# Sums of weight blocks moved from VectorE to DMA transfers that add to their destination

## The reference, cut to what matters

```python
def swiglu(x, g, w_gate, w_up, w_down):
    n = rms_norm(x, g)
    return (jax.nn.silu(n @ w_gate) * (n @ w_up)) @ w_down
# D_MODEL = 1024, D_FF = 2816, DEPTH = 2; x is 512 + 128 rows
```

## Time and profile before

| | |
|---|---|
| median of three runs | 1427.65 us (1426.31 to 1430.56) |
| profiled execution, its time | 1429.83 us |
| its span in the trace | 1428.5 us |
| TensorE busy | 98% of the span |
| VectorE busy | 74% |
| ScalarE busy | 50% |
| GpSimd busy | 11% |
| granted TensorE clock | full in every slice |
| RUN, layer 0 and 1 | 376.4 to 676.7 us; from 1076 to 1375 us |

### The profile page before, as it was taken

One profiled execution on the slowest core, in us unless ns is written; L12 is line 12 of the kernel. 1 busy time (PEld: TensorE's weight loads), 2 busy tenths in 40 slices (PEclk: granted clock), 3 DMA queues, 4 the chain that ended last, 5 costly groups with the idle time before them and its releaser, 6 DMA issues.

```text
span 1428.5 us, 24281 instructions
## 1 busy us (share of the span) xinstructions
PE 1402.7 (98%) x9340; PEld 1321.5 (93%) x9340; DVE 1061.1 (74%) x1875; ACT 713.0 (50%) x1414; POOL 156.6 (11%) x110
## 2 busy tenths in 40 slices
PE   7999999999999999999999999999999999999998
PEld 6897878999999999999988978699999999999998
DVE  5658667878789889877444776677797998998853
ACT  5458555334355455454444685643344544544534
POOL 2416020210000000000222341102000000000002
PEclk9999999999999999999999999999999999999999
DMA  5330221233022222322233211213221223222312
GB/s 171 109 113 14 74 70 39 81 104 104 30 89 66 89 84 74 104 89 74 74 84 107 85 56 47 77 42 102 79 74 60 82 71 114 62 88 89 111 45 96
DMA packets 148642, 115.25 MB, mean 81 GB/s; under 512 B 17936, under 2 KB 143248, under 8 KB 148496
## 3 DMA queue, kind: packets, MB, share of 16 engines
q1 hardware_dynamic: 148528, 113.71, 26.4%
HBM read 108.90 MB, written 6.62 MB: 81 GB/s over the span
## 4 chain that ended last, share of the span: by engine, by line
PE 86%; DVE 7%; ACT 3%; DMA 1%; issue 1%; SPq 1%; DVEq 0%; ACTq 0%
PE ps L675 23%; PE ps L1359 13%; PE ps L1360 13%; PE ps L1361 13%; PE ps L802 3%; PE ps L804 3%; PE ps L803 3%; PE ps L1236 1%; PE ps L1127 1%; ACT pw L1521 1%; PE ps L728 1%; DMA wraw<-w_uq 1%; DVE ringl L2507 1%; PE ps L917 1%; PE ps L1153 1%
## 5 line engine op out<-in xcount | busy, mean ns | idle before, releaser
L2037 DVE TENSOR_TENSOR wlo<-wraw,whi 128x1024 fp32r<-128x1024 f32 (+2 forms) x87 | 97.6, 1122 | 122.9 <-ACT whi L1475 122.8
L1360 PE MATMUL ps<-tl,ringh 128*128 128x320 f32 x576 | 177.8, 309 | 0.0
L1361 PE MATMUL ps<-tth,ringl 128*128 128x320 f32 x576 | 177.5, 308 | 0.0
L1359 PE MATMUL ps<-tth,ringh 128*128 128x320 f32 x576 | 177.0, 307 | 0.0
L1891 ACT ACTIVATE ringh<-sums 128x512 fp32r<-128x512 f32 (+1 forms) x208 | 123.7, 595 | 106.3 <-DVE sums L2499 35.9
L2507 DVE TENSOR_TENSOR ringl<-sums,ringh 128x512 fp32r<-128x512 f32 (+1 forms) x208 | 134.2, 645 | 9.6 <-ACT ringh L1891 8.2
L1475 ACT ACTIVATE whi<-wraw 128x1024 fp32r<-128x1024 f32 (+2 forms) x87 | 81.0, 936 | 112.5 <-PE ps L675 52.0
L1360 PE MATMUL ps<-tbl,ringh 128*128 128x320 f32 x432 | 133.5, 309 | 0.0
L1361 PE MATMUL ps<-tbh,ringl 128*128 128x320 f32 x432 | 133.4, 309 | 0.0
L1359 PE MATMUL ps<-tbh,ringh 128*128 128x320 f32 x432 | 133.4, 309 | 0.0
L1359 PE MATMUL ps<-dhi,ringh 128*128 128x320 f32 x336 | 105.6, 314 | 5.2 <-DVE dlo_rest L2512 2.8
(11 more groups left out here) (431 smaller groups left out, 3786.4 us busy)
## 6 DMA issues: line engine op xcount, KB each, us to landing
raw_gate<-w_gate SPq DMA_DIRECT2D x18, 1024.0 KB, 5.4
raw_up<-w_up SPq DMA_DIRECT2D x18, 1024.0 KB, 5.3
raw_gate<-w_down SPq DMA_DIRECT2D x8, 768.0 KB, 4.2
raw_up<-w_down SPq DMA_DIRECT2D x8, 768.0 KB, 4.2
wraw<-w_down SPq DMA_DIRECT2D x16, 384.0 KB, 3.3
wraw<-w_out SPq DMA_DIRECT2D x32, 128.0 KB, 2.9
wraw<-w_out SPq DMA_DIRECT2D x16, 256.0 KB, 3.1
wraw<-w_gate SPq DMA_DIRECT2D x8, 512.0 KB, 3.9
```

The lines of the kernel that those rows point to most:

```text
L1359: mm(o, wh[:, c, :], xh[:, c, :], start=fresh and c == 0, stop=False, skip_group_check=True)
L1360: mm(o, wh[:, c, :], xl[:, c, :], start=False, stop=False, skip_group_check=True)
L1361: ins = mm(o, wl[:, c, :], xh[:, c, :], start=False, stop=c == (DP if down else KH) - 1, skip_group_check=True)
L2037: vec.tensor_tensor(wlo[:, w], wraw[:, w], whi[:, w], ALU.subtract).then_inc(unit_lo.sem, 1)
```

## The change

All four sums of a set are made by DMA transfers that GpSimd issues and that add their source to what lies at their destination (`add_block`). Since such a transfer can only add, the sums are redefined without a minus, and the signs move to the right operands and to the emptying of PSUM:

- 5: a21 + a22, in the place of a21
- 6: (a21 + a22) + a11, in the place of a11, so only once the low part of product 1 is made
- 3: a12 + sum 6, in `extra` slot 0, into which a fresh copy of a12 is loaded
- 7: a11 + a21, in `extra` slot 1, into which a11 is loaded; its other term, a21, comes from DRAM

SyncE's queue gets two more loads for each set (`load_extra`, 256 KB each, 192 KB for down). `left_sums` is gone from VectorE. Sign changes turn some `tensor_tensor` into `scalar_tensor_tensor` with scalar -1 (`minus_sum`, `up_c21`), and two ScalarE activations get a scale of -1. In the down sets, other than the first of a block, products 3 and 2 change places. The first ring entry waits for the last plain unit (`U_DOWN`) instead of the middle of it. Some semaphores are merged (`tables_in` into `consts_in`, `out_y` and `out_copy` into `out_last`).

```diff
@@ down_products
-        yield n, 3
-        yield n, 2
+        for x in (3, 2) if n == first else (2, 3):
+            yield n, x
@@
-    pair_in = [sig("left_in0", 16 * (len(LEFTS) // 2)), sig("left_in1", 16 * (len(LEFTS) // 2))]
+    pair_in = [sig("left_in0", 48 * (len(LEFTS) // 2)), sig("left_in1", 48 * (len(LEFTS) // 2))]
+    sum_in = {x: sig(f"left_sum_in{x}", 16 * len(LEFTS)) for x in (5, 6, 3, 7)}
@@ left_of
-        return {1: block_of(n, 0, 0), 2: block_of(n, 1, 0), 4: block_of(n, 1, 1), 5: sum_of(n, 0), 6: sum_of(n, 1),
-                3: sum_of(n, 0), 7: sum_of(n, 1)}[x]
+        return {1: block_of(n, 0, 0), 2: block_of(n, 1, 0), 4: block_of(n, 1, 1), 5: block_of(n, 0, 1), 6: block_of(n, 0, 0),
+                3: extra_of(n, 0), 7: extra_of(n, 1)}[x]
@@ sync
+            def load_extra(q):
+
+                n = LEFTS[q]
+                landed, value = left_landed(n)
+                sp.wait_ge(landed, value(l))
+                if q == 0:
+                    sp.wait_ge(unit_used.sem, unit_used.at(l, U_DOWN))
+                else:
+                    sp.wait_ge(a_lo.sem, a_lo.at(l, STEP[LEFTS[q - 1], 3] + 1))
+                sp.dma_start(extra_of(n, 0), left_source(l, n, 1, 0)).then_inc(pair_in[q % 2].sem, 16)
+                if q:
+                    sp.wait_ge(a_lo.sem, a_lo.at(l, STEP[LEFTS[q - 1], 7] + 1))
+                sp.dma_start(extra_of(n, 1), left_source(l, n, 0, 0)).then_inc(pair_in[q % 2].sem, 16)
@@
             for q in range(2, len(LEFTS)):
+                load_extra(q - 1)
                 load_left(q)
+            load_extra(len(LEFTS) - 1)
@@ scalar, left_high
-                    act.wait_ge(a_sum.sem, a_sum.at(l, 4 * PLACE[n] + {5: 1, 6: 2, 3: 3, 7: 4}[x]))
+                    act.wait_ge(sum_in[x].sem, sum_in[x].at(l, 16 * (PLACE[n] + 1)))
@@
-                    act.wait_ge(n_freed.sem, n_freed.at(l, 1))
+                    act.wait_ge(unit_used.sem, unit_used.at(l, U_DOWN))
@@ vector
-                        left_sums(*RUN[i + AHEAD])
                         left_low(*RUN[i + AHEAD])
@@ gpsimd, ahead of the layer's last sum_squares
+            def add_block(x, to, block):
+
+                pool.dma_start(to, block, accum_op=ALU.add).then_inc(sum_in[x].sem, 16)
+
+            for q, n in enumerate(LEFTS):
+                landed, value = left_landed(n)
+                pool.wait_ge(landed, value(l))
+                add_block(5, left_of(n, 5), block_of(n, 1, 1))
+                pool.wait_ge(sum_in[5].sem, sum_in[5].at(l, 16 * (q + 1)))
+                pool.wait_ge(a_lo.sem, a_lo.at(l, STEP[n, 1] + 1))
+                add_block(6, left_of(n, 6), left_of(n, 5))
+                pool.wait_ge(landed, value(l) + 32)
+                add_block(7, left_of(n, 7), left_source(l, n, 0, 1))
+                pool.wait_ge(sum_in[6].sem, sum_in[6].at(l, 16 * (q + 1)))
+                add_block(3, left_of(n, 3), left_of(n, 6))
```

More of the change, by code:

```diff
@@ L188, in hybrid_encoder_step @@
     _, nn, _, ts = place(H0, [("skip_nn", [P, 4 * T], F32), ("nn", [P, 4, HALF], F32), ("skip_ts", [P, 4 * T], F32), ("ts", [P, 4, HALF], F32)])
-    ringh, sums2, ringl, raw_up = place(20480, [("ringh", [P, RING, KH * P], F32R), ("sums2", [P, 2, KH, P], F32),
+    ringh, extra, ringl, raw_up = place(20480, [("ringh", [P, RING, KH * P], F32R), ("extra", [P, 2, KH, P], F32),
                                                 ("ringl", [P, RING, KH * P], F32R), ("raw_up", [P, NC_, 2 * P], F32)])
@@ L421, in block_of, with extra_of, left_source @@
         return raw_of(n)[:, rows:2 * DP:2, tile * P:(tile + 1) * P]
[L423 to L425 removed]
+    def extra_of(n, i):
+        return extra[:, i, 0:KH if n < NG else DP, :]
     def left_of(n, x):
[L429 to L430 removed]
+        return {1: block_of(n, 0, 0), 2: block_of(n, 1, 0), 4: block_of(n, 1, 1), 5: block_of(n, 0, 1), 6: block_of(n, 0, 0),
+                3: extra_of(n, 0), 7: extra_of(n, 1)}[x]
+    w_gate, w_up, w_down = (a[name].rearrange("l (k p) n -> l p k n", p=P) for name in ("w_gate", "w_up", "w_down"))
+    def left_source(l, n, rows, tile):
+        if n < NG:
+            w, f = w_up if n % 2 else w_gate, PLAIN + n // 2 * 2 + tile
+            return w[l][:, KH * rows:KH * rows + KH, f * P:(f + 1) * P]
+        b, g = divmod(n - NG, KH)
+        f, d = TILE0[b + 1], 2 * g + tile
+        return w_down[l][:, f + rows:f + 2 * DP:2, d * P:(d + 1) * P]
     def down_low(first, end):
@@ L640, in _ @@
                 load_down(0, d)
+            load_extra(0)
             load_left(1)
@@ L1930, in emptied @@
                     act.wait_ge(up_c21.sem, up_c21.at(l, pair))
-                    run(tg[:, 1, half(0)], ps[:, bx, 0:HALF], ACT.Silu).then_inc(silu_new.sem, 1)
+                    run(tg[:, 1, half(0)], ps[:, bx, 0:HALF], ACT.Silu, scale=-1.0).then_inc(silu_new.sem, 1)
                 elif up and not in_rows and x in (2, 7, 4):
@@ L2458, in right_rows, with minus_sum @@
                                          op0=ALU.mult, op1=ALU.mult).then_inc(right_new.sem, 1)
+            def minus_sum(out, x, y):
+                return vec.scalar_tensor_tensor(out=out, in0=x, scalar=-1.0, in1=y, op0=ALU.mult, op1=ALU.subtract)
             def right_sums(k):
@@ L2603, in emptied @@
                     dve.wait_ge(kept.sem, kept.at(l, KEPT[n, 5]))
-                    vec.tensor_tensor(dst[:, 1, half(1)], ps[:, bx, 0:HALF], k5[:, :], ALU.add).then_inc(c_new.sem, 1)
+                    vec.tensor_tensor(dst[:, 1, half(1)], k5[:, :], ps[:, bx, 0:HALF], ALU.subtract).then_inc(c_new.sem, 1)
                     if up:
@@ L2627, in emptied @@
                     dve.wait_ge(silu_new.sem, silu_new.at(l, PLAIN + SILU[2 * pair, 4]))
-                    vec.tensor_tensor(tu[:, 1, half(0)], ps[:, bx, 0:HALF], tg[:, 1, half(0)], ALU.mult).then_inc(up_c21.sem, 1)
+                    vec.scalar_tensor_tensor(out=tu[:, 1, half(0)], in0=ps[:, bx, 0:HALF], scalar=-1.0, in1=tg[:, 1, half(0)],
+                                             op0=ALU.mult, op1=ALU.mult).then_inc(up_c21.sem, 1)
                     if not in_rows:
```

73 lines of the change are left out of this document (22 added, 51 removed).

## The result

The changed kernel takes **1771.6 us** (1767.8 to 1774.2, 4 runs) where the kernel before takes 1427.0 beside it (1425.4 to 1430.6, 4 runs): a ratio of 1.241, with a 95% interval from 1.2375 to 1.244. The forecast was 1507 with a range up to 1650, so the direction was right and the size was not even in the range. The profiled execution has a span of 1769.9 us, 341.4 more than before.

The account below looks back on a forecast made before the run. TensorE, 98% busy, was taken as the bound; late add chains cost 40 us in gate and up sets, 22 in down sets, 20 behind down sets, less 3 for freed VectorE: 1507 us by the median, range 1423 to 1650.

Parts of the forecast that it names:

- What bounds: Whole kernel: TensorE, busy 98%, is the bound; 133 us less VectorE work can bring at most 5.1 us, 3 taken.
- L: Time of one adding transfer, GpSimd's release to ScalarE's: 4.4 us, 4.1 in down sets; bounds 3.0 and 6.1.
- Add 7 is not in the chain but runs beside add 6.: GpSimd's adds in each set: add 7 lies outside the chain of adds 5, 6, 3 and was given no cost.
- The last sentence of the prediction: GpSimd: forecast wrong if its own span for one add exceeds 3 us, four per 12.3 us set making it the bound.
- Three adds from the landing of the set, room 10.7 us, of which half is lost: Gate and up sets: three adds of 4.4 us exceed 10.7 by 2.5; half lost in 32 sets, 40 us.
- at the start of RUN: First set of RUN: add 6 goes once the first low part is made, about 365; chain covered by 6 us.
- Nothing for the clock: TensorE's matmuls: the forecast's sum has no term for a lower granted clock.
- The DMA engines as a bound: Rival: loads and adds need 11.5 to 16.7 us of 16 engines per 12.3 us set; 1638 us; chance 0.18 including L over 6.1.
- Hidden: Rival: L of 3.1 us or less hides the adds; 1427, or 1424 under 2.7; chances 0.18 within 4 us, 0.12 full gain.
- the Trainium skill's 2.6 us: Skill's rule for a GpSimd transfer, 2.0 us plus bytes over 436 GB/s: 2.6 us for 256 KB, under every room.
- The second citation: Skill's rule that transfers share 16 engines whoever issues them: load, extra loads and adds lengthen each other, pushing L up.
- The one-answer edits: Extra loads covered, scalar forms some 2 us of hidden VectorE time, activation scales free; product 3's new place widens down room from 8.3 to 9.6.

Follow-up runs that it names:

- 5: Changed kernel with 2560 instead of 2048 bytes of descriptor room and without the addition of sum 7: 1574.6 us, ratio 1.103.
- 2: Changed kernel in its 2048 bytes of descriptor room, without the addition of sum 7 (product 7 reads only block a11): 1585.7 us, ratio 1.111.
- 1: Changed kernel with 2560 instead of 2048 bytes of each partition for the descriptors of GpSimd's transfers: 1670.6 us, ratio 1.170.
- 6: Changed kernel in its 2048 bytes, GpSimd's four transfers of a set made plain copies that add nothing (sums left out): 1534.4 us, ratio 1.075.
- 4: Changed kernel with 2560 bytes of descriptor room and add 3 issued ahead of add 7: 1609.8 us, ratio 1.128.
- 8: Kernel before with the new signs alone, its four sums still made by VectorE: 1428.7 us, ratio 1.0001.
- 10: 9 without its adding transfer: the extra load of a11 stays and VectorE adds a21 to it: 1431.7 us, ratio 1.0025.
- 7: Changed kernel with 2560 bytes of descriptor room, product 3 before product 2 again in the down sets: 1689.2 us, ratio 1.179.
- 9: Kernel before with the new signs, only sum 7 made by an adding transfer (one extra load), VectorE making 5, 6 and 3: 1455.2 us, ratio 1.019.
- 12: 9 with one wait more: SyncE issues the next set's load only when sum 7 of the set ahead has landed: 1470.2 us, ratio 1.029.
- 3: Changed kernel in its 2048 bytes of descriptor room, with add 3 issued ahead of add 7: 1800.7 us, ratio 1.261.

## Why the prediction was right or wrong

*What bounds.* TensorE at 98%, at most 5 us to gain from VectorE: right. Nothing was gained anywhere. VectorE's busy time fell to 955.8, by 105 us and not by the 131 of the forecast (133 less 2): I multiplied 208 sums by their full duration, while neighbours in a row start 0.6 us apart with durations of 0.69 and overlap, so a sum removed gave back 0.5 on average.

*L.* Near: 4.4 forecast, 4.2 to 5.2 found from issue to landing, and both bounds held (3.0 below, 6.1 above) as long as one add is in flight. With two, 8.2. But L was defined from release to release, and in the chain of 5 the two adds took 5.0 and 5.7 us by it, and 0.6 more ahead of the first: 11.3 us where the forecast has 8.8. Not foreseen at all is that GpSimd can't issue the next add meanwhile.

*"Add 7 is not in the chain but runs beside add 6."* This is the step that failed. It was put at nothing and costs 186 us at 2048 bytes (2), or 197 together with the larger room (the changed kernel against 5), of 344. It is in no chain of data, but in GpSimd's line: the next add isn't issued until room is free, 4.5 us or more behind the one before, and with 2560 bytes 1.6 us behind (1). The last sentence of the prediction had this case, GpSimd over 3 us for an add, as what would make it wrong, but tied it to GpSimd's own span. That is 1.3 us; the rest of the slot of 4.5 us stands ahead of the instruction as "issue". A reader who looks only at the span finds the prediction confirmed.

*Three adds from the landing of the set, room 10.7 us, of which half is lost.* Right that the sums come too late at product 6 once they are transfers, wrong in where the chain begins and ends. The loop that runs goes from sum 3 to sum 3 of the next set, through ScalarE's list and the low part of 1, with two adds in it, and takes 15.2 us a set (5), where the forecast has 13.5. The landing of the set, from which the forecast counted, releases only add 5, which is not in the loop; what I said of add 6 and the first low part "at the start of RUN" holds in 49 of 52 sets. TensorE's waits in 5 are 101 us, 96 more than before, against 82 forecast. That this is so near is luck: a wrong chain with a small L and half of the excess lost came out like the right one. With copies the two differ: some 20 us by the forecast's sum, 107 measured (6).

*Nothing for the clock.* In 5 TensorE is busy 1449.8 us, 47 more than before; in the changed kernel 93. The forecast has no term for it, which is its second failed step. At 93 us for 248 of stall, its 82 would have cost 31 more, and 40 by the 47 for 96 in 5: some 1540 to 1550, nearer to what its own world takes (1574.6).

*The DMA engines as a bound.* The forecast's sum for a set was 11.5 to 16.7 us of all 16 engines. Measured in the changed kernel: 0.73 x 20.39 = 14.9. With room for two adds (4), a set of 16.7 us has this row:

```profile
424.79:441.48 16.69, 12.87 (x76) 12.61 (x75) 11.42 (x22) 7.38 (x16) 5.21 (x5) 0.82 0.90 162
```

0.90 x 16.69 = 15.0 us again, and in the set ahead of it (409.70 to 424.79) the share is 0.95, 14.3 us. As long as a gate set needs 14 to 15 us of the engines with four adds, it can't be had in 12.3, whatever their order. Even without add 7 (5) they are busy 0.81 of the 15.17 us from 419.20 on, 12.3 us, as long as a whole set before. I gave this rival its price of 1638 us and a chance of 0.18, and the price lies between the times of 4 and 1 (1609.8 and 1670.6). In the changed kernel the room for descriptors hid it. How much of 4 is this bound and how much is the late add 5, no run separates.

*Hidden.* It fell on both counts, the landing (4.4, not under 3.1) and the reasoning that transfers of 2.7 us or less hide the chain is in doubt: by the Trainium skill's 2.6 us the forecast would be 1424; the kernel of 6, in which two of three transfers of the chain land in 2.8 and the third in 5.6 or 4.3, takes 1534.

*The second citation* (the Trainium skill, "DMA: Bandwidth & Descriptors", section "Issuing engines are not separate DMA queues"), that transfers share the 16 engines whoever issues them: the trace agrees, 7.8 against 4.2 us for the same addition with and without a load beside it (9, 12). The same section says that more issuing engines save only the time to initiate a transfer, "usually small relative to the DMA itself". Here that differs: with 2048 bytes a second add is issued 4.5 us or more behind the first, about as long as the first takes to land.

*The one-answer edits.* Signs and forms with a scalar: 0 (8), as said. The extra loads: one of a set costs 3 us in all (10), near to the nothing I had; the other, of a12, was not tried alone. The place of 3: open (7). No version tried beats the kernel before.

## What to carry to other kernels

Before work is moved to transfers that GpSimd issues, count the runs (contiguous pieces) of one transfer and how many transfers are to be in flight: a queue without room for a second turns independent transfers into a chain, and the sign is idle time ahead of the instruction that the profile puts down to nothing. Then follow the loop that a step is in from one iteration to the next, through every in-order list on the way, instead of the way from its data's arrival. And where TensorE is at 98%, price a stall at more than its length, here 1.4 to 1.7 times (1.4 in the changed kernel, 1.5 in 5, 1.7 in 6), because the granted clock falls with it.

## What was not expected of the hardware

- An adding transfer makes 489 packets where a copy of it makes 75 (means over 512 and 384 runs of 512 bytes). At 256 KB it lands in 4.2 to 5.2 us against 2.8 with no other transfer of GpSimd in flight, in 7.8 beside a load of 1 MB and in 8.2 behind another add.
- 512 bytes more of descriptor room for each partition are worth 101 us in this kernel, and 11 us where one of four transfers is gone. 2048 bytes hold one add of 512 runs, 2560 hold two, and neither holds one more.
- GpSimd's span for an add (1.3 us) says nothing of how often it can issue one: every 4.5 us at best with room for one, 1.6 us behind the other with room for two.
- The granted clock of TensorE is 1.00 in a set without a stall and 0.82 where TensorE works 14.5 of 21.3 us. Not every stall lowers it: in the set of 5 from 419.20 to 434.37, where TensorE works 13.2 of 15.2 us, it is 1.00.
- Where TensorE stands matters beside how long: in 3 it is idle 5 us less than in the changed kernel, at two places of a set and not one, and its matmuls take 36 us longer. Why is open.
